# The chunk stage of an RWKV-7 layer: joined products, and every head kept in its own rows and columns

## The reference, cut to what matters

```python
def step(state, inp):
    r_t, dec_t, k_t, v_t, kk_t, b_t = inp
    sa = jnp.einsum("bhvk,bhk->bhv", state, kk_t)
    state = (state * dec_t[:, :, None, :]
             - sa[..., None] * b_t[:, :, None, :]
             + v_t[..., None] * k_t[:, :, None, :])
    y_t = jnp.einsum("bhvk,bhk->bhv", state, r_t)
    return state, y_t
```

## Time and profile before

| what | value |
|---|---|
| median of 3 runs (lowest, highest) | 1895.83 us (1889.74, 1896.53) |
| the profiled execution | 1890.53 us, of it 1888.5 us span |
| PE busy over the span | 1477.2 us (78%) |
| DVE, ACT, POOL busy | 1033.5, 802.5, 252.0 us |
| mean granted TensorE clock | 0.877 of 2.4 GHz |
| chunk stage | from 323.4 to 557.5 us of the span, 234.1 us |
| PE busy in it | 159.5 us |

### The profile page before, as it was taken

One profiled execution on the slowest core, in us unless ns is written; L12 is line 12 of the kernel. 1 busy time (PEld: TensorE's weight loads), 2 busy tenths in 40 slices (PEclk: granted clock), 3 DMA queues, 4 the chain that ended last, 5 costly groups with the idle time before them and its releaser, 6 DMA issues. The chain is left out here.

```text
span 1888.5 us, 31222 instructions
## 1 busy us (share of the span) xinstructions
PE 1477.2 (78%) x12741; PEld 1122.4 (59%) x12741; DVE 1033.5 (55%) x1167; ACT 802.5 (42%) x1065; POOL 252.0 (13%) x239
## 2 busy tenths in 40 slices
PE   3899986777741953999999299999985629999991
PEld 2274854666641423788777287777874427888771
DVE  4332545434329133888887523444445339888883
ACT  2123323222221022777776323343531217877771
POOL 1000027323104003011110300000001030101101
PEclk9698995989885986999999599999986759999995
DMA  4041200001125053999997422111100539999984
GB/s 140 18 146 59 90 0 12 15 16 27 26 75 228 0 192 132 379 393 391 393 391 266 167 89 67 47 66 45 46 23 0 192 112 354 391 393 393 392 311 156
DMA packets 162399, 313.20 MB, mean 166 GB/s; under 512 B 30256, under 2 KB 31536, under 8 KB 161520
## 3 DMA queue, kind: packets, MB, share of 16 engines
q1 hardware_dynamic: 149904, 265.36, 39.4%
q0 software_dynamic: 7488, 25.24, 3.7%
q10 hardware_dynamic: 4896, 20.97, 2.7%
HBM read 282.12 MB, written 29.43 MB: 165 GB/s over the span
## 5 line engine op out<-in xcount | busy, mean ns | idle before, releaser
L1126 DVE TENSOR_TENSOR moe_wlo<-moe_raw,moe_whi 128x2048 fp32r<-128x2048 f32 x192 | 436.6, 2290 | 89.6 <-ACT moe_whi L1122 89.4
L1122 ACT ACTIVATE moe_whi<-moe_raw 128x2048 fp32r<-128x2048 f32 x192 | 363.4, 1915 | 42.3 <-DMA moe_raw<-in_moe_w_down_dram 19.7
L1133 PE MATMUL all_bank<-moe_whi,moe_xhi 128*128 128x512 f32 x512 | 207.3, 405 | 4.1 <-DVE moe_xlo L1178 4.1
L1135 PE MATMUL all_bank<-moe_whi,moe_xlo 128*128 128x512 f32 x512 | 201.3, 393 | 0.0
L1134 PE MATMUL all_bank<-moe_wlo,moe_xhi 128*128 128x512 f32 x512 | 201.1, 393 | 0.0
L1133 PEld LDWEIGHTS all_bank<-moe_whi,moe_xhi 128*128 128x128 f32 x512 | 97.3, 190 | 23.6 <-DVE moe_xlo L1178 4.9
L1135 PEld LDWEIGHTS all_bank<-moe_whi,moe_xlo 128*128 128x128 f32 x512 | 97.1, 190 | 21.2
L1134 PEld LDWEIGHTS all_bank<-moe_wlo,moe_xhi 128*128 128x128 f32 x512 | 97.5, 191 | 18.4
L1133 PE MATMUL all_bank<-moe_whi,moe_hhi 128*128 128x512 f32 x256 | 101.9, 398 | 4.4 <-issue 4.4
L1135 PE MATMUL all_bank<-moe_whi,moe_hlo 128*128 128x512 f32 x256 | 101.3, 396 | 0.0
L1134 PE MATMUL all_bank<-moe_wlo,moe_hhi 128*128 128x512 f32 x256 | 101.0, 395 | 0.0
(11 more groups left out here) (358 smaller groups left out, 3042.4 us busy)
## 6 DMA issues: line engine op xcount, KB each, us to landing
moe_raw<-in_moe_w_gate_dram SPq DMA_DIRECT2D x64, 1024.0 KB, 12.2
moe_raw<-in_moe_w_up_dram SPq DMA_DIRECT2D x64, 1024.0 KB, 13.2
moe_raw<-in_moe_w_down_dram SPq DMA_DIRECT2D x64, 1024.0 KB, 11.7
out_dram<-moe_yo ACTq DMA_DIRECT2D x32, 512.0 KB, 6.3
attn_xhat<-in_w_kv_dram SPq DMA_DIRECT2D x10, 1024.0 KB, 5.0
attn_xhat<-in_attn_w_q_dram SPq DMA_DIRECT2D x6, 1024.0 KB, 4.9
all_h<-in_rwkv_w_v_dram SPq DMA_DIRECT2D x4, 1024.0 KB, 7.9
all_h<-in_rwkv_w_k_dram SPq DMA_DIRECT2D x4, 1024.0 KB, 6.4
```

The source lines that it names most:

```text
L1122: nc.scalar.activation(whi[slot % SPLITS][:, :], raw[slot % 6][:, :], ACT.Copy).then_inc(m["hi_ok"], 1)
L1126: nc.vector.tensor_tensor(wlo[slot % SPLITS][:, :], raw[slot % 6][:, :], whi[slot % SPLITS][:, :].bitcast(fp32), ALU.subtract).then_inc(m[ ...
L1133: nc.tensor.matmul(bank[b][:, :], hi[:, k0 + k, :], wh[:, k, :], start=begin and k == 0, stop=False)
L1135: ins = nc.tensor.matmul(bank[b][:, :], lo[:, k0 + k, :], wh[:, k, :], start=False, stop=end and k == 3)
```

## The change

Every head stays in rows and columns `half(b)`: `side` is b, `at_level` is gone, and an ordinary product takes one of two quarters of the array by b. The inverse becomes the third part of `pw`, beside N and its transpose, and one product with 128 columns makes the next transpose and the next inverse term together (L908 after). The inverse is then added by whole operations of 128 partitions. `AR` gets a third part, the identity times the decay at the chunk's end, so that the scores product, now 192 columns wide, gives the transposes that `turned` made; they come out decayed, and the state's own decay moves to POOL (`dec`). The scores go in four rounds over two bank pairs.

```diff
-        side = lambda m, b: b ^ (m // GP)
-        other = lambda m, b: 1 - side(m, b)
-        at_level = lambda m, b, lv: side(m, b) ^ (m // GP & lv & 1)
+        side = lambda m, b: b
+        other = lambda m, b: 1 - b
+        score_bank = lambda rd, kind: bank[4 + 2 * (rd % 2) + kind]
...
+                inc(nc.gpsimd.tensor_tensor(AR[c % 3][:, :, 2, :], spread(g["ident2"][:, :], KT), last(c, every), ALU.mult), "ar_ok")
...
+            def decay(c):
...
+                inc(nc.gpsimd.tensor_tensor(dec[:, :, :], sv[:, :, :], last(c, every), ALU.mult), "dec_ok")
...
+            def square(c, lv):
+                wait(act, "sq_done", c, lv + 1)
+                for gr in range(2):
+                    strip(pw[lv % 2][:, pairs(gr), 0, :], four(bank[2 + gr]), "sq_ok")
+
+            def turned(c, lv, gr):
+                if gr == 0:
+                    wait(act, "pow_done", c, lv + 1)
+                elif lv > 0:
+                    wait(act, "q_ok", c, 2 * (lv - 1) + 1)
+                strip(pw[lv % 2][:, pairs(gr), 1, :], bank[gr][:, :].rearrange("p (m x t) -> p m x t", m=GP, x=2)[:, :, 0, :], "nt_ok")
...
-                    for x in range(2):
-                        inc(nc.vector.tensor_tensor(qb[c % 2][(lv + 1) % 2][half(x), :, :], src[half(x), :, :], qb[c % 2][lv % 2][half(1 - x), :, :], ALU.add), "q_ok")
+                for gr in (1, 0):
+                    new = qf[c % 2][:, pairs(gr), :] if lv == 5 else pw[lv % 2][:, pairs(gr), 2, :]
+                    if gr == 0 and lv < 4:
+                        wait(dve, "nt_ok", c, 2 * lv + 1)
+                    src = bank[gr][:, :].rearrange("p (m x t) -> p m x t", m=GP, x=2)[:, :, 1, :]
+                    inc(nc.vector.tensor_tensor(new, src, pw[(lv - 1) % 2][:, pairs(gr), 2, :], ALU.add), "q_ok")
...
-                    for x in range(2 if lv < 4 else 1):
-                        for m, b in heads:
-                            rows, out = half(at_level(m, b, lv)), half(at_level(m, b, lv + 1))
-                            ins = mm(bank[m // GP][out, cols(m, 128)][:, 64 * x:64 * x + 64], now[rows, m, 1 - x, :], now[rows, m, x, :], start=True, stop=True)
-                    inc(ins, "pow_done")
...
+                rows = out = lambda m, b: half(b)
                 if lv < 5:
                     for m, b in heads:
+                        ins = mm(bank[2 + m // GP][out(m, b), cols(m, 64)], now[rows(m, b), m, 1, :], now[rows(m, b), m, 0, :], start=True, stop=True)
+                    inc(ins, "sq_done")
+                if lv == 1:
+                    wait(pe, "q0_ok", c, 2)
+                elif lv > 1:
+                    wait(pe, "q_ok", c, 2 * (lv - 1))
+                lo, hi = (1, 2) if lv == 0 else (1, 3) if lv < 4 else (2, 3)
+                for m, b in heads:
+                    ins = mm(bank[m // GP][out(m, b), cols(m, 128)][:, 64 * (lo - 1):64 * (hi - 1)], now[rows(m, b), m, 0, :],
+                             now[rows(m, b), m, lo:hi, :].rearrange("p x t -> p (x t)"), start=True, stop=True)
+                inc(ins, "pow_done")
```

More of the change, by code:

```diff
@@ new lines, in decay @@
+            def decay(c):
+                if c >= 1:
+                    wait(pool, "s_ok", c - 1, 2)
+                else:
+                    wait(pool, "setup", 0, 1)
+                inc(nc.gpsimd.tensor_tensor(dec[:, :, :], sv[:, :, :], last(c, every), ALU.mult), "dec_ok")
+            keys(0)
+            inverse_start(0)
+            keys(1)
+            for c in range(NC):
+                decay(c)
+                if c < NC - 1:
+                    inverse_start(c + 1)
+                if c < NC - 2:
+                    keys(c + 2)
@@ L668, in turned, with strip @@
-            def turned(c):
-                if c >= 2:
-                    wait(act, "rec_done", c - 2, 1)
[L671 to L677, removed]
-            turned(0)
+            def strip(dst, src, name):
+                inc(nc.scalar.activation(dst, src, ACT.Copy), name)
@@ new lines, in keys, with level @@
+            def keys(c, rd):
+                if c >= 2 and rd == 0:
+                    wait(act, "rec_done", c - 2, 1)
+                for kind, dst, name, ready in ((0, BT, "bt_ok", "nb_ok"), (1, KTR, "kt_ok", "ks_ok")):
+                    wait(act, ready, c, rd + 1)
+                    strip(dst[c % 2][:, two(rd), :], score_bank(rd, kind)[:, 0:384].rearrange("p (m x t) -> p m x t", m=2, x=3)[:, :, 2, :], name)
+            def level(c, lv):
+                if lv == 0:
+                    square(c, lv)
+                    turned(c, lv, 0)
+                    turned(c, lv, 1)
+                elif lv < 4:
+                    square(c, lv)
+                    turned(c, lv, 0)
+                    turned(c, lv, 1)
+                else:
+                    square(c, lv)
@@ L680, in _ @@
+            for rd in range(4):
+                keys(0, rd)
             for c in range(NC + 1):
                 if c < NC:
-                    power(c, 0, 0)
+                    level(c, 0)
                 if c >= 1:
@@ L685, in _ @@
                     for gr in range(2):
-                        strip(zb[:, pairs(gr), :], 4 + gr, 0, "z_ok")
+                        strip(zb[:, pairs(gr), :], four(bank[4 + gr]), "z_ok")
                 if c < NC:
-                    for gr in range(2):
-                        power(c, 1, gr)
+                    level(c, 1)
                 if c >= 1:
@@ L692, in _ @@
                     for gr in range(2):
[L693 removed]
+                        strip(ub[:, pairs(gr), :], four(bank[4 + gr], 256), "u_ok")
                 if c < NC:
[L695 to L696 removed]
+                    level(c, 2)
                 if c >= 1:
@@ L748, in _ @@
+            for rd in range(4):
+                scores(0, rd)
             lower(0)
```

288 lines of the change are left out of this document (121 added, 167 removed).

## The result

Four runs of the changed kernel have a median of 1872.44 us (1871.19 to 1873.80); four of the kernel before on the same chip 1892.78 (1889.73 to 1896.53). The ratio is 0.989, with an interval of 0.987 to 0.992: about 1.1% faster. On another chip, with five rounds, it was 0.988 (0.986 to 0.990). The profiled executions are 1890.53 us before and 1873.23 after, 17.3 us less; the prediction had 12.7 less and a median of 1883. The sign was right and the time lay in the range, but the gain was larger than forecast: 4.6 us larger by the profiled executions.

A forecast was written before the change was run, and what follows sets the result against it. PE was taken as bound by code arriving each 3.99 us. Steady chunks 23 us less, start 3 more, end 0.7 less, clock 8 more: 12.7 less, 1877.8, plus 5.3 for the median, 1883; range 1867 to 1899.

The forecast's parts named there:

- What bounds the kernel before: Chunk stage: PE's code arrives one packet each 3.99 us, 6.9 packets or 27.5 us a chunk against 27.8 measured.
- The stream: PE in each steady chunk: 22.5 us of streaming plus 1.5 bare waits, 24.0 for 27.8, 23 us less over six.
- the two forecast waits: PE waiting for DVE around a chunk's end: 0.9 us before the next chunk's level 0, 0.4 before level 5.
- code stays the bound: Rival, chance 0.10: with a cheap 128-column product and few clock falls, chunks take 22 us, median near 1866.
- The start: First product, chunk 0 and first part of chunk 1: 3 us more, bounds 1 and 6.
- The end: Chunk 7, the last: 15.2 us against 15.9, 0.7 less.
- The clock: Chunk stage: 16 us at half clock, costing 8 us, bounds 0 and 20.
- likely place: Chunk 0, with bare waits between short groups, named as where a fall to 1.2 GHz could come; no separate size.
- The median: Whole kernel: profiled execution of before lies 5.3 us under its median of three, so 1877.8 becomes 1883.
- Levels wait longer: Rival, chance 0.22: ACT and DVE hand-overs between inverse levels add 1.5 us a chunk, 12 in all, near 1895.
- Code was never the bound: Rival, chance 0.03: chunk stage keeps its idle time and the wider stream adds 52 us, near 1948.
- The clock stays down: Rival, chance 0.10: two-quarter work in level 2, `finish_chunk` and level 3 runs at half clock, 65 us more, near 1940.

The follow-up runs named there:

- the short products: Kernel before with 64 more products of 4 columns a chunk, ahead of the powers of levels 1 to 4: 1921.87 us, ratio 1.017.
- the third chip: Kernel before, changed kernel and two four-quarter versions rerun on one more chip, five rounds: before 1893.80 us, changed 1872.47 us, ratio 0.988.
- the pause experiment: Changed kernel with six useless DVE operations at each chunk's end, ahead of level 5 of the inverse: 1895.58 us, ratio 1.003.
- the version with short products after: Changed kernel with 64 more products of 4 columns a chunk, ahead of the squares of levels 1 to 4: 1901.68 us, ratio 1.009.

## Why the prediction was right in kind and short in size

*What bounds the kernel before: right.* That code arrives every 4 us and sets the pace was read from one trace; the experiments bear it out. More instructions with hardly any columns lengthen a chunk by 3.3 us, of which 1.8 at most are PE's own time, and on four quarters 48 fewer products for the same columns shorten it by 3.3. The forecast of a chunk from its instructions alone (products x 4 / 260 x 3.99) was 21.6, 24.6 and 31.4 us for 352, 400 and 512 products; measured 22.28, 25.56 and 31.16. A rival that the prediction left out is that PE takes some 15 ns for each instruction (3.99 us / 260) for a reason of its own, however early the code is there: it would give the same sums. The trace of before speaks against it. PE doesn't run evenly slow, it stands, and at other times starts 64 records with their weight loads in a microsecond, 8 ns an instruction. And it starts again at much the same time after a packet. Two stands, with the DMA view of 392 to 400 us (40 slices of 0.2 us; the packets are the 82, at 392.2 and 396.0; the last slices are other transfers):

```profile
GB/s 0 82 0 0 0 0 0 0 0 0 0 0 0 0 0 0 0 0 0 0 82 0 0 0 0 0 0 23 182 153 12 0 45 160 123 8 182 110 36 179
394.96 0.21 PE L866 MATMUL all_bank<-chunks_ub,chunks_bt 64*64 64x64 f32 x1 [0.84 <-issue]
398.82 0.32 PE L900 MATMUL all_bank<-chunks_qb,chunks_pw 64*64 64x64 f32 x2 [1.31 <-issue]
```

They end 2.7 and 2.8 us after a packet started. In the six chunks of before PE stands 40 times for over 0.5 us, beside 43 packets, and 34 of these stands end 2.1 to 3.0 us after a packet has started; if they had nothing to do with packets, some 9 would. With the short products it is 41 of 47.

*The stream: right, with errors that are small and partly cancel.* Forecast 22.5 us of stream and 1.5 of bare waits. Measured 23.0 busy and 1.25 idle (7.5 us in six), of which 1.1 are the two forecast waits, at the two forecast places, 0.8 and 0.3 for 0.9 and 0.4. The joined product is 53 ns for the 56 taken; its lower bound of 29 did not come, and with it goes "code stays the bound". Six chunks give 21.3 us for 23; of the difference 1.1 is the one chunk of 25.2, which holds the "issue" wait of 0.8.

*The start: 4.0 us for 3, inside its bounds, with the parts off.* The stretch before the first product is 1.1 us longer (2.1 forecast for the operation on POOL and the score rounds), and the stage is entered 0.5 later. Chunk 0 is 2.4 longer, not 3.4. But the first part of chunk 1, 14.6 us, gives back nothing where I counted 1.6. *The end*: 0.1 less for 0.7.

*The clock: this step failed.* The prediction's step was: "I take 16 us at half clock, about the share of before, 8 us". There is no time at half clock after, from the first product to the last state update, neither here nor on the third chip, so the term is 0. Without it the prediction's sum was 20.7 us less, against 17.3 measured; with it 12.7. The 8 us were too much, and it was luck that the other terms promised 3.4 us more than came: without that the sum would have missed by 8 us and not by 4.6. The term was wrong in how often a fall comes, not in what one costs: in the pause experiment a fall of 3.4 us costs 1.3, near the 1.7 (half of 3.4) that I reckoned with. It wasn't the share of before either: a mean of 0.92 over 181.4 us is about 29 us at half clock. The rows that I quoted had each fall behind a stretch in which PE was idle for most of the time, 2.0 and 2.3 of 3.4 us. My own working left 1.5 us of bare waits a chunk, in two pieces, and measured are 0.8 us at a chunk's end, with PE busy for 2.56 of the 3.4 us around it. No row of mine had a fall behind so short a wait, so in the steady chunks the forecast should have been hardly any.

What makes a fall come stays open. The pause of 2.8 us brings one each time; the version on four quarters with products taken apart is idle for 27% without one; but the version with short products after has one behind a wait of 1.0 us in chunk 0. So my "likely place", chunk 0, was not a bad guess, though no fall came there in the changed kernel. In the kernel before the two falls of the earlier trace rows follow a wait of 2.0 us that the profile puts down to `qb` on DVE (L842) and an "issue" wait of 1.9. Both end 2.8 to 2.9 us after a packet started, so late code may be behind both (the packet at 384.4 in the earlier trace rows and the stand that ends at 387.4 are the first).

*The median.* The prediction added 5.3 us, since the profiled execution of before lay that far under the median of three. With a fourth run of before that distance is 2.3 us, and after the change the profiled execution lies 0.8 above its median. The distance was chance, and it makes up 6.0 us of the miss in the median.

*The rivals.* "Levels wait longer" did not come: in the six chunks PE waits for no copy of ACT in the rows above. "Code was never the bound" is out by the short products in the kernel before. "The clock stays down" is out by the trace and by the pause.

## What to carry to other kernels

When an engine waits at changing lines with no releaser, count its instructions between the packets of its code queue before looking at dependencies: here one packet each 4 us was the floor, and where it was the bound, 48 fewer products for the same columns were worth 3.3 us a chunk, more than any wait. See also whether the stands end at the same time after a packet. Then work out the next bound beside it, since it caps the gain: going to two quarters gave back 1.4 to 1.8 us of every chunk that fewer products had won, and keeping four quarters with the joined product was faster than both kernels. Price a clock fall by the waits behind which it would have to come in the new kernel, not by the share of time it had before, and give the term a wide range.

## What the runs showed of the hardware beyond that

- A product of 4 columns on a 64x64 quarter takes as long as one of 64 (1.05 and 1.13 us for 32 records on two quarters), one of 128 nearly twice (53 against 28 ns a record).
- In the pause experiment a stretch at 1.2 GHz with products on two quarters of the array, PE busy for 3.03 of 3.4 us, was followed by full clock.
- At half clock products on two quarters take nearly twice as long: 32 records in 1.97 us in the pause experiment, against 1.10 at full clock in the changed kernel:

```profile
388.27 1.97 PE L903 MATMUL all_bank<-all_h 64*64 64x64 f32 x32 [2.76 <-DVE chunks_qf L777]
```

- A wait that the profile puts down to DVE can have late code behind it: the waits for `qf` on four quarters went over into "issue" when `qf` came earlier, with the chunk nearly unchanged (22.28 and 22.33 us; on the third chip 22.70 and 22.44).
- In a long stretch code packets for PE came no closer together than 3.9 us on average: 3.88 (43 in 167.0 us of the kernel before) to 4.13 us in the versions where "issue" waits are many, and up to 4.82 (34 in 164.0 us, with the pause) where there are next to none.
